# FFN gate and up of a one-layer hybrid encoder step: seven block products over token halves in place of eight over three token chunks

## What is computed

```python
def _swiglu(x, w_gate, w_up, w_down):
    return (jax.nn.silu(x @ w_gate) * (x @ w_up)) @ w_down
...
x = x + 0.5 * _swiglu(_rmsnorm(x, g_f1), w_g1, w_u1, w_d1)
h = _rmsnorm(x, g_mix)
... # one projection; a gated convolution, forgetting attention and memory attention; x = x + mix @ w_out
x = x + 0.5 * _swiglu(_rmsnorm(x, g_f2), w_g2, w_u2, w_d2)
x = _rmsnorm(x, g_fin)
```

## Time and profile before

| what | us |
|---|---|
| three runs | 2353.02, 2360.74, 2362.45 |
| median | 2360.74 |
| profiled execution, first to last instruction (span) | 2353.5 |
| TensorE busy of it | 2230.7 (95%) |
| DVE, ACT, POOL busy | 809.3, 576.3, 616.2 |

### The profile page before, as it was taken

One profiled execution on the slowest core, in us unless ns is written; L12 is line 12 of the kernel. 1 busy time (PEld: TensorE's weight loads), 2 busy tenths in 40 slices (PEclk: granted clock), 3 DMA queues, 4 the chain that ended last, 5 costly groups with the idle time before them and its releaser, 6 DMA issues.

```text
span 2353.5 us, 35745 instructions
## 1 busy us (share of the span) xinstructions
PE 2230.7 (95%) x13627; PEld 2138.4 (91%) x13627; DVE 809.3 (34%) x1812; ACT 576.3 (24%) x1101; POOL 616.2 (26%) x409
## 2 busy tenths in 40 slices
PE   5999999999999989899999989879999999999997
PEld 4899999999999979879888777679999999999996
DVE  4312222211222273445544555662221122222125
ACT  4311111111111241152433433541111111111113
POOL 4322223332223421221121213232333221233310
PEclk8999999999999999899999999989999999999997
DMA  5110111111111012402020110111111101111001
GB/s 163 54 37 18 53 53 53 53 36 39 32 53 54 0 30 35 61 29 68 9 77 23 54 49 19 41 54 54 54 53 53 36 18 53 53 53 53 18 9 74
DMA packets 149843, 107.80 MB, mean 46 GB/s; under 512 B 13400, under 2 KB 139608, under 8 KB 149792
## 3 DMA queue, kind: packets, MB, share of 16 engines
q1 hardware_dynamic: 149792, 107.11, 16.7%
HBM read 97.84 MB, written 9.25 MB: 46 GB/s over the span
## 4 chain that ended last, share of the span: by engine, by line
PE 53%; DVE 4%; ACT 2%; issue 2%; another core or an unknown queue 0%; POOL 0%; DVEq 0%; ACTq 0%
PE banks L228 15%; PE banks L229 14%; PE banks L230 14%; PE banks L1472 3%; PE banks L1511 3%; PE banks L1492 2%; PE banks L1423 1%; DVE row_bias L1180 1%; DVE h_f L1016 1%; DVE xT L1102 0%; DVE w_raw L1249 0%; ACT norm_squares L721 0%; PE banks L1521 0%; ACT mprobs L885 0%; PE banks L1579 0%
## 5 line engine op out<-in xcount | busy, mean ns | idle before, releaser
L228 PE MATMUL banks<-h_hi,w_hi 128*128 128x384 f32 (+1 forms) x2592 | 857.0, 331 | 45.9 <-DVE h_lo L1010 24.6
L229 PE MATMUL banks<-h_lo,w_hi 128*128 128x384 f32 (+1 forms) x2592 | 842.1, 325 | 0.0
L230 PE MATMUL banks<-h_hi,w_lo 128*128 128x384 f32 (+1 forms) x2592 | 839.8, 324 | 0.0
L228 PEld LDWEIGHTS banks<-h_hi,w_hi 128*128 128x128 f32 x2592 | 490.4, 189 | 57.5 <-issue 37.0
L229 PEld LDWEIGHTS banks<-h_lo,w_hi 128*128 128x128 f32 x2592 | 491.7, 190 | 3.2
L230 PEld LDWEIGHTS banks<-h_hi,w_lo 128*128 128x128 f32 x2592 | 491.1, 189 | 0.0
L577 POOL TENSOR_TENSOR act_lo<-act_f,act_hi 128x384 fp32r<-128x384 f32 x132 | 125.1, 948 | 1049.1 <-ACT act_hi L767 1049.1
L1032 DVE TENSOR_TENSOR act_f<-silu,banks 128x384 f32<-128x384 f32 x132 | 68.8, 521 | 929.6 <-PE banks L230 925.2
L1038 DVE SCALAR_TENSOR_TENSOR xT<-banks,xT 128x384 f32<-128x384 f32 (+1 forms) x528 | 277.0, 525 | 233.2 <-PE banks L230 233.2
L228 PE MATMUL banks<-act_hi,wd_hi 128*128 128x384 f32 (+1 forms) x1056 | 342.6, 324 | 0.0
L229 PE MATMUL banks<-act_lo,wd_hi 128*128 128x384 f32 (+1 forms) x1056 | 341.0, 323 | 0.0
(11 more groups left out here) (190 smaller groups left out, 1942.6 us busy)
## 6 DMA issues: line engine op xcount, KB each, us to landing
w_raw<-in_w_ffn_gate SPq DMA_DIRECT2D x44, 512.0 KB, 4.9
w_raw<-in_w_ffn_up SPq DMA_DIRECT2D x44, 512.0 KB, 6.2
wd_raw<-in_w_ffn_down SPq DMA_DIRECT2D x44, 512.0 KB, 4.2
w_raw<-in_w_in SPq DMA_DIRECT2D x20, 512.0 KB, 6.5
minusF<-negF_rows SPq DMA_DIRECT2D x8, 592.0 KB, 4.7
x_by_token<-in_x_prompt SPq DMA_DIRECT2D x8, 512.0 KB, 6.2
w_raw<-in_w_out SPq DMA_DIRECT2D x8, 512.0 KB, 6.6
out_y_prompt<-w_raw SPq DMA_DIRECT2D x8, 512.0 KB, 2.6
```

The costliest lines, as they stand in the source:

```text
L228: eng.matmul(out, w_hi, x_hi, start=first, stop=False)
L229: eng.matmul(out, w_hi, x_lo, start=False, stop=False)
L230: return eng.matmul(out, w_lo, x_hi, start=False, stop=last)
```

## The change

Gate and up of 256 hidden features and 528 tokens (`HALF`) are now computed as a 2 x 2 by 2 x 2 block product: the weight is cut into two halves of hidden features and two halves of the 1024 inputs, `h` into two halves of inputs and two quarters of tokens (`QC` = 264). Seven products of blocks, with sums of blocks as operands, give what eight gave. Each is 4 k-blocks x 3 matmuls of 264 columns, 84 for gate and 84 for up. An FFN has 22 iterations i (NI) in place of 11 groups: 11 for the first half of the tokens, 11 for the second. Down is 16 products e of 6 matmuls of 264 columns, in banks 6 and 7; gate has banks 0 to 2, up 3 to 5.

The sums are new work. Of the weights, DVE makes four sums of 512 columns for gate and four for up (`sums`), and the low parts of these sums (`sums_lo`, 2 x 1024 columns each); ACT makes the high parts in five pieces each (`part_hi`: 512, 1024, 512, 1024, 512 columns), POOL the low parts of the three unsummed pieces (`part_lo`, 512 columns each). Slots 3 to 6 of the split weights are shared by gate and up. Of `h`, DVE makes the seven forms once for each half (`forms`: two scaled copies of 528 columns and four sums of 264, for each of 4 kk), ACT their high parts (7 x 264), POOL five low parts (1320 columns), DVE two (`forms_lo2`). Of the results, DVE adds the banks together (`combine`, five steps of 264), with a copy by ACT (`first_copy`). Weights are loaded and split once for each half, so twice for an FFN. The norm of the second half is taken in iterations NF-3 and NF-2.

```diff
-                group(0, True)
-                with pe.Fori(1, NF) as g:
-                    group(g, False)
+                f, i0 = FFN, NI * n
+                for i in range(i0, i0 + NI):
+                    if i == i0 + NF:
+                        down_product(n, i - 1)
+                    pair_product(n, "gate", i)
+                    if i == 0:
+                        for t in XG[2]:
+                            x_turn(t)
...
+                    if i % NF:
+                        down_product(n, i - 1)
...
+                    pair_product(n, "up", i)
+                down_product(n, i0 + NI - 1)
```

```diff
+            def pair_product(n, which, i):
...
+                    if i and q in (1, 2):
+                        pe.wait_ge(C, 5 * i)
...
+                    if q == 3:
+                        pe.wait_ge(f[f"{which}_m1"], i + 1)
+                    if q in (4, 5, 6):
+                        pe.wait_ge(C, 5 * i + (2, 2, 3)[q - 4])
...
+            def down_product(n, i):
...
+                for e in range(16):
+                    c, d = divmod(e, KT)
+                    if 16 * i + e >= 2:
+                        pe.wait_ge(f["resid"], 16 * i + e - 1)
```

The order of DVE in an iteration (second half's start first):

```diff
+                    if i == i0 + NF:
+                        forms_lo2(f, 2 * n + 1, 0)
+                        forms(n, 1, 2)
+                        forms_lo2(f, 2 * n + 1, 1)
+                        for e in range(4):
+                            add_down(f, i - 1, e)
+                        forms(n, 1, 3)
+                        for e in range(4, 8):
+                            add_down(f, i - 1, e)
+                        forms_lo2(f, 2 * n + 1, 2)
+                        forms_lo2(f, 2 * n + 1, 3)
+                        for e in range(8, 16):
+                            add_down(f, i - 1, e)
+                    sums_lo(f, "gate", i, 1)
+                    combine(f, "gate", i, 0)
+                    combine(f, "gate", i, 1)
+                    sums(f, "up", i, 0)
+                    combine(f, "gate", i, 2)
+                    sums(f, "up", i, 1)
+                    combine(f, "gate", i, 3)
+                    combine(f, "gate", i, 4)
+                    sums_lo(f, "up", i, 0)
...
+                    tail = [lambda: sums_lo(f, "up", i, 1)]
+                    if i + 1 < i0 + NI:
+                        tail += [lambda: sums(f, "gate", i + 1, 0), lambda: sums(f, "gate", i + 1, 1),
+                                 lambda: sums_lo(f, "gate", i + 1, 0)]
...
+                        for e in range(16):
+                            add_down(f, i - 1, e)
+                            if e in (1, 4, 6, 9) and tail:
+                                tail.pop(0)()
...
+                    combine(f, "up", i, 0)
+                    combine(f, "up", i, 1)
+                    combine(f, "up", i, 2)
+                    multiply(f, i, 0)
+                    multiply(f, i, 3)
+                    combine(f, "up", i, 3)
+                    multiply(f, i, 1)
+                    combine(f, "up", i, 4)
+                    multiply(f, i, 2)
+                    if i == i0 + EARLY_I:
+                        forms(n, 1, 0)
+                        forms(n, 1, 1)
```

Both inputs of `sums`, `sums_lo`, `forms` and of `multiply` for q > 0 lie in SBUF, for example:

```diff
+                    dve.tensor_tensor(SS[:, 0, :], A21, A22, ALU.add).then_inc(S, 1)
...
+                dve.tensor_tensor(slots(wlo, wxl, slot, 2), SS[:, 2 * part:2 * part + 2, :],
+                                  slots(whi, wxh, slot, 2).bitcast(F32), ALU.subtract)\
```

More of the change, by code:

```diff
@@ L182, in hybrid_step @@
         x0 = semaphores("x0", "loaded0 loaded1 loaded2 turned copied_lo copied_hi")
-        FFN = [semaphores(f"ffn{n}", "loaded_a loaded_b dloaded hi_a hi_b lo_a lo_b dhi dlo gate_done up_done silu_done "
-                    "act_made act_hi act_lo down_done resid") for n in (1, 2)]
-        NORM = [semaphores(f"norm{n}", "squares sums mean rough dve hi lo") for n in (1, 2, 3)]
+        FFN = semaphores("ffn", "gate_loaded up_loaded down_loaded gate_sums up_sums gate_hi up_hi down_hi "
+                          "gate_lo up_lo gate_sums_lo up_sums_lo down_lo gate_done up_done gate_m1 up_m1 gate_c up_c "
+                          "silu prod act_hi act_lo down_done resid forms forms_hi forms_lo forms_lo2")
+        NORM = [semaphores(f"norm{n}", "squares sums mean rough dve" + " hi lo" * (n == 2)) for n in (1, 2, 3)]
         fg = semaphores("forget", "wloaded wsplit proj dve act past turned copied stored")
@@ L359, in _ @@
                 sp.dma_start(bfor[:, :], i["b_forget"][0].rearrange("(p a) -> p a", a=1)).then_inc(s_small, 16)
[L361 to L382, removed]
+            load_up(0)
             load_x(2)
-            load_gu(0, 0, 1)
             sp.wait_ge(x0["turned"], 2 * NT)
+            load_down(0)
             ffn_loads(0)
@@ L558, in norm_sums @@
                 pool.tensor_tensor(nsum[:, 0:w], nsq[:, 0, 0:w], nsq[:, 1, 0:w], ALU.add).then_inc(N["sums"], 1)
[L560 to L575, removed]
-                    pool.wait_ge(f["act_hi"], 6 * g + u + 1)
-                    pool.tensor_tensor(actl[:, j, s:s + w], actf[:, u % 2, 0:w], acth[:, j, s:s + w].bitcast(F32),
-                                       ALU.subtract).then_inc(f["act_lo"], 1)
-                    if more and c == 2:
-                        gu_lo(n, g + 1, j)
@@ new lines, in first_copy, with silu_11 @@
+            def first_copy(f, which, i):
+                act.wait_ge(f[f"{which}_done"], 7 * i + 1)
+                if which == "up":
+                    act.wait_ge(f["gate_c"], 5 * i + 5)
+                elif i:
+                    act.wait_ge(f["up_c"], 5 * i)
+                act.activation(ca[:, :], bank(0 if which == "gate" else 3, QC), ACT.Copy).then_inc(f[f"{which}_m1"], 1)
+            def silu_11(f, i):
+                act.wait_ge(f["gate_done"], 7 * i + 4)
+                if i:
+                    act.wait_ge(f["prod"], 4 * i)
+                act.activation(gq[:, 0, :], bank(0, QC), ACT.Silu).then_inc(f["silu"], 1)
@@ L1042, in _ @@
+            for t in XG[0] + XG[1]:
                 x_copy(t)
@@ L1330, in _, with half_mean @@
-            for t in range(NT):
+            def half_mean(n, c, b):
+                N = NORM[n]
+                if c < 2:
+                    pe.wait_ge(N["squares"], c + 1)
+                    for k in range(KT):
+                        mm = pe.matmul(bank(b, QC), onesD[:, :], FT[:, c % 2, k, :], start=k == 0, stop=k == KT - 1)
+                    mm.then_inc(N["mean"], 1)
+                    return
+                pe.wait_ge(N["sums"], 3 * (c - 1))
+                pe.matmul(bank(b, QC), onesD[:, :], FT[:, c % 2, 4, :], start=True, stop=True).then_inc(N["mean"], 1)
@@ L1568, in _ @@
             pe.wait_ge(LOOPS["mem"]["resid"], 24 * ITER["mem"] + 4)
+            for c in range(2):
+                half_mean(2, c, 6 + c)
             ffn(1)
```

583 lines of the change are left out of this document (419 added, 164 removed).

## The result

| | before | after |
|---|---|---|
| median, us | 2357.57 (4 runs, 2353.02 to 2362.45) | 2561.45 (4 runs, 2555.76 to 2564.89) |
| ratio, with its 95% interval | | 1.086 (1.0836 to 1.0884) |
| profiled execution: time / span | not listed apart / 2353.5 | 2559.3 / 2557.5 |

The change makes the kernel **8.6% slower**: 204 us, where 182 was forecast (2543 against the 2360.74 of the runs shown). The page of the kernel after, engine shares and granted clock in 40 slices; the same lines of before are the earlier trace rows.

The account below looks back on a forecast made before the run. TensorE, 95% busy, bounds the kernel; 3.06 us less matmul time an iteration is outweighed by 5.7 stalled. An FFN is 849.5 less 767, 91 more with the start; twice, +182 gives span 2535.7, time 2543, range 2405 to 2605.

Parts of the forecast that it names:

- The pace of TensorE: Matmuls of 264 columns take 0.1205 us each, so an unstalled iteration is 31.8 us, 3.06 less than before.
- The stall of an iteration: Down's two banks and POOL holding DVE stall TensorE 5.7 us, making an iteration 37.5 us against 34.87 before.
- What POOL costs: DVE instructions with two SBUF inputs and POOL instructions reading SBUF exclude each other; without it an iteration is 35.5 us.
- case A: DVE and POOL hold each other up less: iteration 35.5 us, change of halves 25, start 3; 2423 us, chance 0.2.
- The change of halves: Between token halves, down's adds stand behind `forms`, which alternate with POOL's 3.0 us pieces; gate starts at 37.5 us.
- The starts: At each FFN's start, `forms` alternating with POOL's low parts delay the first products; 8.5 us an FFN.
- The first iterations of a half: Two iterations an FFN have no down between gate and up and take 20.2 us each.
- the loads costed at nothing: Doubled weight loads, 3 MB an iteration, are issued some 10 us before their split at 80 GB/s and cost nothing.
- Squares and mean: In the second half's norm, TensorE waits for the table change and first copy; 5 us an FFN, between 0 and 10.
- Case C: TensorE, idle 15% in short pieces, isn't kept at clock 1.00; 2655 us, or 2600 at 0.96; chance 0.1.
- Case B: DVE's tails in down are absorbed, with no stall within an iteration; faster, 2257 us, chance 0.1.

Follow-up runs that it names:

- the ninth experiment: Four banks, reordered edges and late sums, plus gate's combines 2 and 3 between up's sums and ACT's down-weight copy earlier in a half's first iteration; 2368.13 us, ratio 1.004.
- experiment 2: Against the kernel after: down goes through four banks (4 to 7) in place of 6 and 7, DVE's work and order unchanged; 2455.24 us, ratio 1.041.
- experiment 1: Against the kernel after: POOL's low parts of weights and act replaced by memsets of zeros that read nothing, `forms` keeping its own; 2501.55 us (one run).
- experiment 5: Against the kernel after: down in four banks, and POOL's low parts of weights and act replaced by memsets that read nothing; 2368.49 us (one run).
- experiment 6: Against the four-bank kernel: at the change of halves the sixteen adds are spread between the forms and their low parts; 2456.61 us, ratio 1.0422.
- experiment 4: Against the kernel after: gate sums and most `sums_lo` cover 16 columns a slot in place of 512, outside an FFN's first iteration; 2442.91 us (one run).

## Why the prediction was right, and where a size was off

The case that happened is the forecast, 18 us above its 2543 and inside the range. By its steps:

- **The pace of TensorE.** 0.1215 us a matmul for 0.1205, so 32.1 an unstalled iteration for 31.8. Over columns / 2.4 GHz that is 11.5 ns, within the 9 to 16 of the rows. Right: the gain was there to be had, 2.8 us an iteration, and the ninth experiment takes 2.6 of it.
- **The stall of an iteration.** 37.5 forecast, 36.96 measured, at every interval but those with squares, mean or an edge, within 0.03. Over 40 iterations that is 21 us less than forecast. The places were right: five waits, at the head and at each tail, and a small one in gate (0.45 by the starts, 0.20 in its bracket, forecast 0.6). The two causes, and what each measured: two banks 2.43 us (experiment 2), POOL 1.17 (experiment 1), both together 4.32 of 4.9 (experiment 5). That they make more together than one by one fits waits that they share.
- **What POOL costs.** The mechanism stood on a single row and held for the two-input operations in general (195 of the 197 counted above). The Trainium skill (SBUF — State Buffer, "Who interferes with whom") adds that POOL instructions that only write don't take part; experiment 1 agrees, with the second sum at 0.69 us beside memsets in the fifth experiment against 1.78 with four banks and POOL's subtractions. But the price of the whole was put at 120 us (2543 less case A's 2423) and measured 60. Three terms were too high. An iteration was to be 2.0 us shorter without the exclusion, 80 us in all; it was 1.17 shorter, 47 us. The change of halves was to fall from 37.5 to 25 us; it fell from 39.6 to 35.1, since `forms_lo`, which experiment 1 keeps, goes on taking turns with `forms`; over the two FFNs that is 9 us in place of 25. The starts were to be 5.5 us shorter each; the first isn't (DVE's first combine at 62.0 us for 61.9), with the same `forms_lo` beside it. How it would be with none of POOL's reads wasn't tried.
- **The first iterations of a half: the mis-sized term.** The prediction put them at 20.2 us, unstalled, and 27.2 for the very first with its tiles. They measured 29.8, 29.5, 28.8 and 40.3: 40.5 us more in all. The step that failed is that it costed DVE and POOL in the iterations with a down stretch, and ran these two by TensorE alone. The cover that was gone is down: ACT's copy of up's first bank stands behind the sums of the next gate. In the very first iteration, 13 of the 40.5 us, a second step failed with it, the loads costed at nothing: DVE and ACT wait 8.4 and 9.8 us for the second gate load, and TensorE 11.1 behind them where in the other three it waits 6.3. How much of the 13 us is the load's alone wasn't tested.
- **The change of halves.** 37.5 forecast, 39.6 measured (76.6 us from gate to gate less an iteration), 4 us in all. The explanation given, adds behind `forms`, holds only for where TensorE is seen to wait; experiment 6 spreads them and gains 1.6 us. The chain below it is what counts (DVE `forms`, ACT, POOL `forms_lo`), as the alternation of 3 us pieces in the forecast had it.
- **Squares and mean.** 5 an FFN taken, 2.2 measured, 6 us less in all.

Sum of these: -21 + 40.5 + 4 - 6 = +18. The profiled span is 22 over the forecast span of 2535.7; the 4 us left are in starts, ends and the middle. Some 2 are at the first start, where DVE's first combine comes at 61.9 us and the forecast start of 57 with 24 matmuls makes 59.9; the rest wasn't followed up. The profiled execution stands 2 us over its span, the median 4, where 7 was added. **Case C** (a slower clock): its premise fails in the iterations, where the granted clock is 1.00 in spite of waits of 0.3 to 1.0 us, but not at the edges. Length, busy time by engine and granted clock of a first iteration and of the change of halves in the kernel after:

```profile
1671.23:1701.01 29.78, 23.25 (x171) 22.86 (x171) 17.72 (x27) 11.38 (x17) 12.23 (x7) 0.85 0.37 107
2035.91:2112.53 76.62, 52.61 (x363) 50.41 (x362) 54.94 (x87) 20.11 (x24) 31.02 (x14) 0.82 0.14 42
```

The forecast took 1.4 us per long wait for the clock; here it can't be told apart from the waits. **Case B** (faster) fell with the two banks: DVE's chain was in fact tighter than taken (a pair of adds lasts 0.77, so 0.34 apart, for 0.40), as that case wanted, but tails of 1.1 to 1.5 us don't fit between products of 0.73.

## What to carry to other kernels

Fewer products on the bound engine are worth what the helpers can hide: follow one pass in order of time, and ask at each add how far TensorE can run ahead; depth in banks (two to four) gave 106 us here at no cost in work, where leaving out most of the tails gave 119. Where DVE has two inputs in SBUF, place it away from POOL's reads: the same sums some two microseconds later, behind POOL's pair, were worth 59 us, while a fifth less tail work elsewhere was worth nothing. And cost the passes that lack a stage (first, last, at a change) by themselves, since the missing stage is the cover of the others' order.

## What the runs showed of the hardware that was not expected

- What a DVE instruction costs under the exclusion is set by what is left of POOL's instruction, not by its own size: 16 columns took 0.91 us in the mean where POOL held them and 0.16 where not, and 264 columns 4.81 us under POOL's 2048. It goes the other way too: POOL's pieces of 512 columns last 1.30 alone and up to 2.3 behind DVE.
- With two banks in turn, the adds of experiment 4 start 0.76 us apart where the product takes 0.73, 0.03 us a product with nothing between the adds. That this is the round trip from TensorE to DVE and back is argued, not shown.
- The reported wait of a stalled matmul (the brackets sum to 2.85 us in a down stretch) is less than the time lost by the marks of the stages (26.75 against 21.9 between gate and up).
